# Attention tiles in pairs of two heads, with one barrier per pair and the value products issued head by head

## What is computed

```python
s = einsum('bshe,bmhe->bhsm', q, km) * HEAD_DIM ** -0.5     # memory heads, 256 keys each
p = softmax(s);  o = einsum('bhsm,bmhe->bshe', p, vm)
s = where(band_mask, einsum('bdnqhe,bdnkhe->bdnhqk', q, k) * HEAD_DIM ** -0.5, NEG)   # dilated heads
p = exp(s - logsumexp(s));  o = einsum('bdnhqk,bdnkhe->bdnqhe', p, v)
```

## Time and profile before

| what | value |
|---|---|
| three runs | 2153.06, 2160.37, 2160.22 us (median 2160.22) |
| the profiled execution's own time | 2154.56 us |
| its span, first to last instruction | 2152.8 us |
| mean granted TensorE clock | 0.988 |
| attention of layer 0 on TensorE | 69 to 200 us from the span's start |
| attention of layer 1 on TensorE | 990 to 1433 us |

### The profile page before, as it was taken

The page is one execution under the profiler, slowest core; times in us unless marked ns, Lnnn a source line. Parts: engine busy times, 40 slices in busy tenths (PEclk is TensorE's granted clock), DMA queues, the critical chain, the costliest instruction groups (busy, mean ns, idle before and its releaser), DMA issues.

```text
span 2152.8 us, 25437 instructions
## 1 busy us (share of the span) xinstructions
PE 2080.7 (97%) x9458; PEld 1677.7 (78%) x9458; DVE 1469.7 (68%) x2080; ACT 955.5 (44%) x1514; POOL 340.8 (16%) x188
## 2 busy tenths in 40 slices
PE   7998999999999999999999998999999999999997
PEld 6776887888888878887777775678788888888886
DVE  6558676576788676665444465577969988885665
ACT  5335353455555353433455555765622222234441
POOL 3633100111211000000000032020033333310001
PEclk9999999999999999999999998999999999999998
DMA  4218741355787876482111100113236654477544
GB/s 169 95 45 308 264 155 40 140 214 204 260 294 268 327 271 218 157 325 102 60 42 57 63 26 30 40 55 123 82 141 225 234 208 159 174 283 262 192 173 155
DMA packets 119900, 357.39 MB, mean 166 GB/s; under 512 B 10848, under 2 KB 12256, under 8 KB 114528
## 3 DMA queue, kind: packets, MB, share of 16 engines
q1 hardware_dynamic: 103312, 325.59, 42.3%
q10 hardware_dynamic: 16464, 30.15, 4.0%
HBM read 241.28 MB, written 114.43 MB: 165 GB/s over the span
## 4 chain that ended last, share of the span: by engine, by line
PE 76%; DVE 9%; DMA 5%; ACT 5%; issue 4%; SPq 1%; POOL 0%; ACTq 0%; POOLq 0%; DVEq 0%
PE PS L954 10%; PE PS L953 10%; PE PS L955 10%; PE PS L721 8%; PE PS L726 7%; PE PS L722 7%; PE PS L971 5%; PE PS L973 5%; PE PS L972 5%; PE PSC L870 3%; PE PO L842 2%; DMA inner<-TP 1%; DMA TP<-x_mid 1%; PE PTR L852 1%; DMA RR<-inner 1%
## 5 line engine op out<-in xcount | busy, mean ns | idle before, releaser
L971 PE MATMUL PS<-RP,DH 128*128 128x512 f32 x616 | 241.3, 392 | 2.7 <-DVE RP L2207 2.7
L972 PE MATMUL PS<-RP,DH 128*128 128x512 f32 x616 | 240.4, 390 | 0.0
L973 PE MATMUL PS<-RP,DL 128*128 128x512 f32 x616 | 240.3, 390 | 0.0
L954 PE MATMUL PS<-BLT,SH 128*128 128x512 f32 x576 | 224.1, 389 | 0.0
L955 PE MATMUL PS<-BHT,SL 128*128 128x512 f32 x576 | 224.1, 389 | 0.0
L953 PE MATMUL PS<-BHT,SH 128*128 128x512 f32 x576 | 224.1, 389 | 0.0
L953 PE MATMUL PS<-BH,SH 128*128 128x512 f32 x432 | 168.2, 389 | 0.7 <-DVE SL L2108 0.7
L955 PE MATMUL PS<-BH,SL 128*128 128x512 f32 x432 | 168.1, 389 | 0.0
L954 PE MATMUL PS<-BL,SH 128*128 128x512 f32 x432 | 168.1, 389 | 0.0
L971 PEld LDWEIGHTS PS<-RP,DH 128*128 128x128 f32 x616 | 115.9, 188 | 27.6 <-DVE RP L2207 3.8
L1088 ACT ACTIVATE DH<-DR 128x1408 fp32r<-128x1408 f32 x56 | 77.3, 1380 | 133.1 <-DMA DR<-s_keep 86.9
(11 more groups left out here) (331 smaller groups left out, 4827.2 us busy)
## 6 DMA issues: line engine op xcount, KB each, us to landing
SR<-in_wst SPq DMA_DIRECT2D x36, 1024.0 KB, 4.9
ZS<-in_wdn SPq DMA_DIRECT2D x32, 704.0 KB, 5.8
s_keep<-ZS SPq DMA_DIRECT2D x32, 704.0 KB, 4.7
DR<-s_keep SPq DMA_DIRECT2D x32, 704.0 KB, 5.4
inner<-TP SPq DMA_DIRECT2D x36, 512.0 KB, 4.2
WR<-in_w SPq DMA_DIRECT2D x35, 512.0 KB, 5.7
DR<-in_wdn SPq DMA_DIRECT2D x24, 704.0 KB, 4.9
RR<-t_keep SPq DMA_DIRECT2D x16, 1024.0 KB, 5.2
```

The lines of the kernel that those rows point to most:

```text
L954: MM(BANK[bank], SH[b][:, w, c], BL[t][:, k, :], start=False, stop=False)
L971: MM(bank, wh[:, i, :], rh, start=(i == 0), stop=False)
L972: MM(bank, wh[:, i, :], rl, start=False, stop=False)
L973: ins = MM(bank, wl[:, i, :], rh, start=False, stop=(i == KD - 1))
```

## The change

Tiles are renumbered: the two heads of a block are neighbours (even tile head 0, odd tile head 1). TensorE handles them in pairs: in an even step it issues the value products of both tiles `a-4` and `a-3`, head by head, each with only its head's 64 columns as weights and 64 rows of output; then the scores of both tiles `a` and `a+1`, after one wait for the exponentials of all tiles before; and then, in every step, the transposes of tile `a-2`, which now come last. Scores of odd tiles go to a bank PSD that takes the place of PO; PO becomes the upper half of the bank PTR. The output copy takes two blocks of both heads (128 partitions by 256) in place of four blocks of one head (64 by 512). The transposes of every fourth tile wait for that copy (`o_free`), since they write the bank that the copy reads.

```diff
         def tile_of(a):
-            sl, h, n = a // 16, (a // 8) % 2, a % 8
+            sl, h, n = a // 16, a % 2, a % 16 // 2
...
         def score_bank(a):
-            return BANK[3] if a > TWO_BANKS and a % 2 else BANK[4]
+            return BANK[6] if a % 2 else BANK[4]
+        QUAD = 2 * P
+        PO = PTR[:, QUAD:2 * QUAD]
...
# step() on TensorE
-                if begin <= a - 3 < end:
-                    b = a - 3
-                    pe.wait_ge(pt_done, b + 1)
+                if begin <= a - 3 < end and a % 2 == 0:
+                    b = a - 4
+                    pe.wait_ge(pt_done, b + 2)
                     if b % 4 == 0 and b:
                         pe.wait_ge(o_free, b // 4)
-                    for i in range(nk // P):
-                        v = VM[:, 2 * i + t - NMT, :] if kind == "mem" else VF[(sl - 3) % 2][:, k0 // P + i, :]
-                        ins = MM(PO[:, P * (b % 4):P * (b % 4 + 1)], v, PT[l][:, b % 2, P * i:P * (i + 1)],
-                                 start=(i == 0), stop=(i == nk // P - 1))
-                    ins.then_inc(pv_done, 1)
-                if begin <= a - 2 < end:
-                    b = a - 2
-                    pe.wait_ge(p_normed, b + 1)
-                    if b:
-                        pe.wait_ge(pt_done, b)
-                    for i in range(nk // P):
-                        ins = nc.tensor.transpose(PTR[:, P * i:P * (i + 1)], PR[l][:, b % 2, P * i:P * (i + 1)], IDENT)
-                    ins.then_inc(p_tr, 1)
-                if a < end:
+                    for h in range(2):
+                        rows = slice(DH * h, DH * (h + 1))
+                        for i in range(nk // P):
+                            v = VM[:, 2 * i + t - NMT, rows] if kind == "mem" \
+                                else VF[(sl - 3) % 2][:, k0 // P + i, rows]
+                            ins = MM(PO[rows, P * (n % 2):P * (n % 2 + 1)], v, PT[l][:, h, P * i:P * (i + 1)],
+                                     start=(i == 0), stop=(i == nk // P - 1))
+                            if i == nk // P - 1:
+                                ins.then_inc(pv_done, 1)
+                if a < end and a % 2 == 0:
...
                     if a:
-                        pe.wait_ge(exp_done, a - 1 if a > TWO_BANKS else a)
-                    MM(score_bank(a)[:, 0:nk], QF[rows, t, P * n:P * (n + 1)], keys,
-                       start=True, stop=True).then_inc(scored, 1)
+                        pe.wait_ge(exp_done, a)
+                    for h in range(2):
+                        rows = slice(DH * h, DH * (h + 1))
+                        keys = KM[rows, t - NMT, :] if kind == "mem" else KF[(sl - 3) % 2][rows, k0:k0 + nk]
+                        MM(score_bank(a + h)[:, 0:nk], QF[rows, t, P * n:P * (n + 1)], keys,
+                           start=True, stop=True).then_inc(scored, 1)
+                if begin <= a - 2 < end:
+                    b = a - 2
+                    pe.wait_ge(p_normed, b + 1)
+                    if b:
+                        pe.wait_ge(pt_done, b)
+                    if b % 4 == 0 and b > begin:
+                        pe.wait_ge(o_free, b // 4)
+                    for i in range(nk // P):
+                        ins = nc.tensor.transpose(PTR[:, P * i:P * (i + 1)], PR[l][:, b % 2, P * i:P * (i + 1)], IDENT)
+                    ins.then_inc(p_tr, 1)
...
# step() on ScalarE
                     if kind == "mem":
-                        A(OF[rows, t, HALF[half]], PO[rows, :], ACT.Copy).then_inc(o_free, 1)
+                        A(OF[:, t, QUAD * (n // 2):QUAD * (n // 2 + 1)], PO, ACT.Copy).then_inc(o_free, 1)
                     else:
                         g = t // 2
-                        A(natural_cols(OF[rows, t, :], g, half), bank_cols(PO[rows, :], g),
-                          ACT.Copy).then_inc(o_free, 1)
+                        A(natural_cols(OF[:, t, :], g, n // 2, 4), bank_cols(PO, g, 4), ACT.Copy).then_inc(o_free, 1)
```

More of the change, by code:

```diff
@@ L486, in build @@
         PTR = ctx.enter_context(nc.psum_tensor("PTR", [P, HT], F32))
-        PO = ctx.enter_context(nc.psum_tensor("PO", [P, HT], F32))
+        PSD = ctx.enter_context(nc.psum_tensor("PSD", [P, HT], F32))
         PX = ctx.enter_context(nc.psum_tensor("PX", [P, HT], F32))
-        BANK = [PS[0][:, HALF[0]], PS[0][:, HALF[1]], PS[1][:, HALF[0]], PS[1][:, HALF[1]], PSC[:, :], PTR[:, :], PO[:, :]]
+        BANK = [PS[0][:, HALF[0]], PS[0][:, HALF[1]], PS[1][:, HALF[0]], PS[1][:, HALF[1]], PSC[:, :], PTR[:, :], PSD[:, :]]
         w_loaded = [sem(f"w_loaded{i}") for i in range(NLOAD)]
@@ L618, in tile_of, with natural_cols, bank_cols @@
             return sl, kind, l, t, h, n, P * (n - 1), 2 * P, (0, 2 * P)
-        TWO_BANKS = 16 * 8
         def score_bank(a):
-            return BANK[3] if a > TWO_BANKS and a % 2 else BANK[4]
+            return BANK[6] if a % 2 else BANK[4]
+        QUAD = 2 * P
+        PO = PTR[:, QUAD:2 * QUAD]
         def by_residue(ap, g):
             return ap.rearrange("p (l r) -> p r l", r=DIL[g])
-        def natural_cols(ap, g, half):
+        def natural_cols(ap, g, i, parts):
+            d, w = DIL[g], S // parts
+            return by_residue(ap, g)[:, i * d // parts:(i + 1) * d // parts, :] if d > 1 else ap[:, w * i:w * (i + 1)]
+        def bank_cols(ap, g, parts):
             d = DIL[g]
[L633 to L638, removed]
+            return ap.rearrange("p (r l) -> p r l", r=d // parts) if d > 1 else ap
         HOOKS = {}
@@ L833, in step @@
                 att["PE"] += 1
-                if begin <= a - 3 < end:
-                    b = a - 3
-                    sl, kind, l, t, h, n, k0, nk, _m = tile_of(b)
-                    pe.wait_ge(pt_done, b + 1)
+                if begin <= a - 3 < end and a % 2 == 0:
+                    b = a - 4
+                    sl, kind, l, t, _h, n, k0, nk, _m = tile_of(b)
+                    pe.wait_ge(pt_done, b + 2)
                     if b % 4 == 0 and b:
                         pe.wait_ge(o_free, b // 4)
-                    for i in range(nk // P):
-                        v = VM[:, 2 * i + t - NMT, :] if kind == "mem" else VF[(sl - 3) % 2][:, k0 // P + i, :]
-                        ins = MM(PO[:, P * (b % 4):P * (b % 4 + 1)], v, PT[l][:, b % 2, P * i:P * (i + 1)],
-                                 start=(i == 0), stop=(i == nk // P - 1))
-                    ins.then_inc(pv_done, 1)
-                if begin <= a - 2 < end:
-                    b = a - 2
-                    l, nk = tile_of(b)[2], tile_of(b)[7]
-                    pe.wait_ge(p_normed, b + 1)
-                    if b:
-                        pe.wait_ge(pt_done, b)
-                    for i in range(nk // P):
-                        ins = nc.tensor.transpose(PTR[:, P * i:P * (i + 1)], PR[l][:, b % 2, P * i:P * (i + 1)], IDENT)
-                    ins.then_inc(p_tr, 1)
-                if a < end:
-                    sl, kind, l, t, h, n, k0, nk, _m = tile_of(a)
-                    rows = slice(DH * h, DH * (h + 1))
+                    for h in range(2):
[8 more added lines that the diff above has]
+                if a < end and a % 2 == 0:
+                    sl, kind, l, t, _h, n, k0, nk, _m = tile_of(a)
                     if a % 16 == 0:
@@ L866, in step @@
                             pe.wait_ge(px_free, px_order["PE"].index(("v", sl - 3, 1)) + 1)
-                    keys = KM[rows, t - NMT, :] if kind == "mem" else KF[(sl - 3) % 2][rows, k0:k0 + nk]
                     if a:
-                        pe.wait_ge(exp_done, a - 1 if a > TWO_BANKS else a)
-                    MM(score_bank(a)[:, 0:nk], QF[rows, t, P * n:P * (n + 1)], keys,
-                       start=True, stop=True).then_inc(scored, 1)
+                        pe.wait_ge(exp_done, a)
[6 more added lines that the diff above has]
+                    b = a - 2
+                    l, nk = tile_of(b)[2], tile_of(b)[7]
+                    pe.wait_ge(p_normed, b + 1)
[6 more added lines that the diff above has]
+                    ins.then_inc(p_tr, 1)
                 if end == A_END and (a - 3) % 16 in (0, 3):
@@ L1182, in step @@
                     sl, kind, l, t, h, n, _, _, _ = tile_of(b)
-                    rows, half = slice(DH * h, DH * (h + 1)), n // 4
                     act.wait_ge(pv_done, b + 1)
                     if kind == "mem":
-                        A(OF[rows, t, HALF[half]], PO[rows, :], ACT.Copy).then_inc(o_free, 1)
+                        A(OF[:, t, QUAD * (n // 2):QUAD * (n // 2 + 1)], PO, ACT.Copy).then_inc(o_free, 1)
                     else:
                         g = t // 2
-                        A(natural_cols(OF[rows, t, :], g, half), bank_cols(PO[rows, :], g),
-                          ACT.Copy).then_inc(o_free, 1)
+                        A(natural_cols(OF[:, t, :], g, n // 2, 4), bank_cols(PO, g, 4), ACT.Copy).then_inc(o_free, 1)
                 if begin <= a - 2 < end:
@@ L1217, in lse_out @@
```

(2 more changed lines are left out.)

## The result

The changed kernel takes 2108.43 us (median of four runs, 2103.86 to 2111.82) against 2159.55 us of the kernel before (four runs): a ratio of 0.9768, 95% interval 0.9740 to 0.9797, some 50 us faster. In a second set of runs the ratio was 0.9787 (0.9774 to 0.9801). The profiled span fell from 2152.8 to 2109.0 us, by 43.8 us.

What follows compares the result with a forecast made beforehand. TensorE was taken to bound the attention stages; -28 (cheaper pairs) + 6 (given back) + 3 (copy waits) + 3 (last stage) = -16 us, so 2143 us forecast, own range 2132 to 2154, the whole 2123 to 2163.

Steps and rivals of the forecast that it cites:

- What bounds the kernel, the price of a step before: Attention stages: TensorE sets the pace; a step costs 0.94 us (single tile) or 1.49 us (double tile).
- Passes: Scores and value products: pass count stays, two heads partly overlap; with form changes, pairs gain 0.53 (double) or 0.40 us (single).
- one pass beside another per group: Scores and value products: only head 0's last and head 1's first pass overlap; 0.11 + 0.22 us per double pair; chance 0.42.
- everything runs side by side: Rival: every pass of one head overlaps one of the other in scores and value products; about -36 us, 2124; chance 0.19.
- Changes of form: TensorE switching between matmul shapes: three changes per pair in place of four, at 0.20 us each.
- How many pairs: TensorE-paced pairs: 12 double in layer 0, 28 double and 17 single in layer 1; 28 us gained; pooling pairs nothing.
- given nothing back: Gain lost to longer waits where TensorE already waits: a quarter of layer 1's 21.6 us, +6 us; none for layer 0.
- The new wait: Every fourth tile's transposes wait for the output copy, 38 times, partly covered by scores; 5 to 10 us of waits, +3 net.
- what I had called wrong: Sign against the forecast: TensorE's waits for the output copy of over 15 us.
- the rival of the shared bank: Rival: transposes waiting for output copies make it slower, +21 us, 2181; decides from 0.5 us per copy; chance 0.14.
- The last stage: From step 123, where cover is thin: no gain, +3 us with its copy waits.
- The chain: From a pair's scores through VectorE and ScalarE to its second exponential: 3.3 us and about 0.2 more, 3.5 per pair.

Runs made afterwards that it cites:

- experiment 1: Changed kernel with the value products issued key block by key block, the two heads in turns: 2107.74 us, ratio 0.9783 to the kernel before.
- experiment 5: Kernel before, with only the value products narrowed to their head's 64 weight columns and 64 output rows: 2186.28 us, ratio 1.0151.
- Experiment 6: Changed kernel; in odd steps VectorE takes the odd tile's maximum before normalising the even one: 2099.81 us, ratio 0.9747; measured again, 2097.23 us, 0.9727.
- serial scores: Changed kernel with head 1's scores made to wait until head 0's have finished: 2134.05 us, ratio 0.9903 to the kernel before.

## Why the prediction was wrong

The direction was right, the size was not: 2143 us forecast, 2123 the low end, 2108 measured. Step by step:

**What bounds the kernel, the price of a step before.** Right. TensorE paced both stages. The pair periods of 7.12 and 5.11 us, less 18 and 14 large matmuls at 0.23 us, are 2.98 and 1.89 us, twice the 1.49 and 0.94. By the same sum a pair now costs 1.84 and 1.18 us, where the prediction looked for 2.4 to 2.5 and 1.5.

**Passes: the step that failed.** I took "one pass beside another per group", arguing that passes start in the order of issue and only neighbours in different halves can overlap. The rows I had could not show this: in the kernel before no two neighbouring products used different halves. In the changed kernel every pass of head 1 runs beside one of head 0, and the order of the value products makes no difference (experiment 1). The term was 0.33 us per double pair (0.11 and 0.22) and 0.22 per single one; it measured 0.86 and 0.43. This is the rival "everything runs side by side", which I gave 0.19. The Trainium skill had it in "TensorEngine Tiling (Array Packing)", "Key Properties": different tiles load weights and multiply in parallel. The trace agrees: eight passes of two heads in 0.66 us, four of one head alone in 0.65 (experiment 5). The other sentence of the Trainium skill that I weighed, in "TensorE: Matmul & The Clock Gate", "Part 3: Packing small matmuls", that matmuls keep program order in start and end, does not hold for the starts between the halves here: head 1's first value product starts at 1002.601, head 0's second product (its third pass) only at 1002.857 us, though that one was issued earlier. The ends in the trace are modelled and say nothing on it.

**Changes of form.** The narrow value products do need a change, as forecast, but 0.20 us was too much for it: in and out of it cost 0.14 us each (experiment 5). A pair saves 0.28 us on its changes, not 0.20, so its three cost 0.52 us together. The direct change from the value products' form to the scores' was not measured by itself.

**How many pairs.** The 57 pairs that TensorE paces would save 40 x 1.14 + 17 x 0.71 = 58 us by the measured prices. By the scores' starts in the two traces, layer 0's 12 pairs brought 9.4 us, not 13.7: waits for exponentials grew by 4.1 us there, where I had given nothing back. Layer 1's pairs from step 32 to the output projection brought 32.8, which is 44 us less 11. That is a quarter, as I had taken it, but by luck: in this stretch the waits for exponentials grew by 3.1 us only, and 9.9 us are waits for the output copy, which I had counted apart.

**The new wait.** I named its place and its cover, and forecast 5 to 10 us of waits; it is 15.7 us, just in what I had called wrong. Over 38 copies that is 0.41 us each, below the 0.5 from which I had let the rival of the shared bank decide, and the gain it is set against came out far larger than the forecast's. I had also said that the waits for the exponential (L1203 then) would shrink. They grew, from 13.9 to 32.5 us.

**The last stage.** The chain was right: 3.5 us per pair by my sum, 3.30 measured, 3.28 before. Experiment 6 confirms it: with the normalising and the wait ahead of it taken out, about 1.0 us (0.49 + 0.50 in my sum), every second pair ran at TensorE's own pace. The stage as a whole, from tile 124's scores to the last pair's, went from 86.8 to 84.2 us, where I had +3.

The rival's time of 2124 us was itself too slow, by the form changes, by a loss of 3 us in the last stage that was a gain of 2.6, and by the 1.7 us that the pooling pairs brought and that I had put at nothing.

## What to carry to other kernels

Two products with a contraction of 64 rows, or with 64 columns of weights, cost here hardly more than one (0.68 against 0.62 us, 0.59 against 0.58) when they use different halves of the array and stand in the same stretch of TensorE's stream. The order within the value products is of no consequence, but a wait between the heads is. The scores of the two heads go to different PSUM banks, the value products to different partitions of one bank; no run here tries other places. A product narrowed without a partner only adds changes of form, 0.14 us each here. After such a gain look at the chain that fed the old pace: here VectorE, which normalises one tile before it reduces the next, held up every second pair of single tiles in the last stage, and swapping the two brought another 12.5 us beside the change (4 to 9 by the first set).

## What the hardware showed that I had not expected

Float32 products of two passes interleave between the halves pass by pass, 6 to 7 ns apart in the scores and 6 to 14 ns in the value products, with a full accumulation group of head 0 (two products, four passes) ahead of head 1's in the stream. A wait of TensorE on its own semaphore between two products of the same form costs 0.33 us in the serial scores' timeline, 0.25 to 0.31 by the pair periods. And a later start is not always a loss: letting head 0's scores go early split 13 pairs and cost 7 us of TensorE's time, about what the shorter waits brought.
